# Hybrid sparse-attention and HGRN2 block: sums of x squares as 32-token products of one column, and ScalarE's order at three places

## What is computed

```python
def rms_norm(x, g):
    xf = x.astype(jnp.float32)
    y = xf * lax.rsqrt(jnp.mean(xf * xf, axis=-1, keepdims=True) + EPS)
    return (y * g.astype(jnp.float32)).astype(x.dtype)

mod = c_act @ w_ada[l] + b_ada[l]
shift1, scale1, gate1, shift2, scale2, gate2 = jnp.split(mod, 6, axis=-1)
h = rms_norm(x, norm1_g[l]) * (1.0 + scale1[:, None]) + shift1[:, None]
proj = h @ w_in[l]
(q_lat, a_k, a_v, k_idx, w_idx, b_q, b_f, b_i, b_g, gate_a, gate_b) = split_cols(proj, COL_SIZES)
q_lat = rms_norm(q_lat, q_lat_norm_g[l])
...
k_idx = rms_norm(k_idx, k_idx_norm_g[l])
...
h2 = rms_norm(x, norm2_g[l]) * (1.0 + scale2[:, None]) + shift2[:, None]
y = jnp.square(jax.nn.relu(h2 @ w_mlp1[l] + b_mlp1[l])) @ w_mlp2[l] + b_mlp2[l]
x = x + gate2[:, None] * y
```

## Time and profile before

| | before |
|---|---|
| median of 3 runs (lowest to highest), us | 771.15 (770.37 to 771.26) |
| the profiled execution's own time, us | 771.27 |
| its span, first to last instruction, us | 769.4 |
| TensorE busy | 761.0 us (99%) |
| VectorE busy | 630.9 us (82%) |
| ScalarE busy | 364.7 us (47%) |
| GpSimd busy | 62.7 us (8%) |
| moved by DMA | 95.50 MB, 124 GB/s on average |

### The profile page before, as it was taken

One profiled execution on the slowest core, in us unless ns is written; L12 is line 12 of the kernel. 1 busy time (PEld: TensorE's weight loads), 2 busy tenths in 40 slices (PEclk: granted clock), 3 DMA queues, 4 the chain that ended last, 5 costly groups with the idle time before them and its releaser, 6 DMA issues.

```text
span 769.4 us, 13224 instructions
## 1 busy us (share of the span) xinstructions
PE 761.0 (99%) x5208; PEld 645.8 (84%) x5208; DVE 630.9 (82%) x1129; ACT 364.7 (47%) x577; POOL 62.7 (8%) x64
## 2 busy tenths in 40 slices
PE   7999999999999999999999999999999999999998
PEld 6876878777878777778889988889999888889998
DVE  6975999778998677769966999879998766779996
ACT  5466524455344376654332555654333354454341
POOL 5015344200000000000012000000000000000000
PEclk9999999999999999999999999999999999999999
DMA  9943223221221233345556255312333433213331
GB/s 349 403 140 110 83 83 107 75 67 56 80 86 58 85 107 126 145 142 184 200 180 203 83 165 191 109 55 86 108 110 109 138 110 102 89 55 111 110 110 56
DMA packets 27643, 95.50 MB, mean 124 GB/s; under 512 B 3009, under 2 KB 3393, under 8 KB 27586
## 3 DMA queue, kind: packets, MB, share of 16 engines
q1 hardware_dynamic: 27296, 94.51, 36.8%
q10 hardware_dynamic: 290, 0.20, 0.1%
HBM read 92.61 MB, written 2.10 MB: 123 GB/s over the span
## 4 chain that ended last, share of the span: by engine, by line
PE 94%; DVE 3%; ACT 2%; issue 1%; DMA 1%; DVEq 0%; ACTq 0%
PE bank L1612 10%; PE bank L1614 10%; PE bank L1613 10%; PE bank L2187 7%; PE bank L2189 7%; PE bank L2188 7%; PE bank L1662 5%; PE bank L1841 2%; PE bank L1798 2%; PE bank L1842 2%; PE bank L1843 2%; PE bank L2015 2%; PE bank L1800 2%; PE bank L1799 2%; PE bank L2017 2%; PE bank L2016 2%
## 5 line engine op out<-in xcount | busy, mean ns | idle before, releaser
L1612 PE MATMUL bank<-h_hi,w_hi 128*128 128x512 f32 x328 | 128.2, 391 | 0.6 <-ACT relu_u L886 0.6
L1613 PE MATMUL bank<-h_lo,w_hi 128*128 128x512 f32 x328 | 127.7, 389 | 0.0
L1614 PE MATMUL bank<-h_hi,w_lo 128*128 128x512 f32 x328 | 127.6, 389 | 0.0
L526 ACT ACTIVATE w_hi<-w_raw 128x1024 fp32r<-128x1024 f32 (+2 forms) x94 | 97.4, 1039 | 30.7 <-PE bank L1819 9.4
L1087 DVE TENSOR_TENSOR w_lo<-w_raw,w_hi 128x1024 fp32r<-128x1024 f32 x68 | 83.5, 1236 | 11.7 <-ACT w_hi L526 11.7
L1612 PEld LDWEIGHTS bank<-h_hi,w_hi 128*128 128x128 f32 x328 | 61.6, 188 | 13.4 <-ACT relu_u L886 0.8
L2187 PE MATMUL bank<-u_hi,wf_hi 128*128 128x256 f32 x256 | 72.6, 284 | 0.1
L2189 PE MATMUL bank<-u_hi,wf_lo 128*128 128x256 f32 x256 | 72.4, 283 | 0.0
L2188 PE MATMUL bank<-u_lo,wf_hi 128*128 128x256 f32 x256 | 72.4, 283 | 0.0
L1614 PEld LDWEIGHTS bank<-h_hi,w_lo 128*128 128x128 f32 x328 | 61.6, 188 | 12.9
L1613 PEld LDWEIGHTS bank<-h_lo,w_hi 128*128 128x128 f32 x328 | 61.6, 188 | 12.6
(11 more groups left out here) (319 smaller groups left out, 1890.4 us busy)
## 6 DMA issues: line engine op xcount, KB each, us to landing
w_raw<-in_units SPq DMA_DIRECT2D x117, 512.0 KB, 3.3
ada_raw<-in_ada SPq DMA_DIRECT2D x16, 512.0 KB, 10.3
ada_even<-in_ada SPq DMA_DIRECT2D x16, 512.0 KB, 4.5
ada_odd<-in_ada SPq DMA_DIRECT2D x16, 512.0 KB, 4.4
w_raw<-in_units SPq DMA_DIRECT2D x8, 448.0 KB, 10.6
xT<-in_xt SPq DMA_DIRECT2D x4, 512.0 KB, 5.3
out<-xT SPq DMA_DIRECT2D x7, 256.0 KB, 2.5
w_raw<-in_units SPq DMA_DIRECT2D x1, 256.0 KB, 5.1
```

Source lines behind the costliest of these rows:

```text
L526: nc.scalar.activation(w_hi[:, s, 0:width], w_raw[:, s, 0:width], ACT.Copy).then_inc(hi_ready, 1)
L1612: mm(bank[b][:], w_hi[:, slot, j], rhs_hi(i), start=f, stop=False)
L1613: mm(bank[b][:], w_hi[:, slot, j], rhs_lo(i), start=False, stop=False)
L1614: end = mm(bank[b][:], w_lo[:, slot, j], rhs_hi(i), start=False, stop=l)
```

## The change

Four edits, in one.

1. The pair sums on VectorE go. Each slice's squares are summed by TensorE on their own, in 16 products of 32 tokens by one column of ones (row_sums), into four columns of bank 7; the root reads these four columns. Behind the first five slices stand two idle products each, behind the sixth one; the idle products behind the spread become seven.
2. VectorE squares slices 5 and 7, ScalarE the other six, and the table load for the root moves ahead of ScalarE's last square.
3. At the latents ScalarE makes both lat_hi, kw and kw_sq first and the latents' squares after these. VectorE's lat_lo now waits for lat_hi alone and its sum for both squares; TensorE waits for a square before it overwrites bank 0.
4. In the first half of the MLP the rounding of the first token-block sums moves from behind unit 1 to behind the relu of unit 2.

```diff
@@ -212,11 +212,12 @@
         ones_ready, consts_ready, consts_step = sem("ones_ready"), sem("consts_ready"), sem("consts_step")
         dve_own, act_own = sem("dve_own"), sem("act_own")
         lb_ready, gqk_ready = sem("lb_ready"), sem("gqk_ready")
-        xsq_ready, xsq_added, xsq_summed, xroot_ready, xspread = (
-            sem("xsq_ready"), sem("xsq_added"), sem("xsq_summed"), sem("xroot_ready"), sem("xspread"))
+        xsq_ready, xsq_made, xsq_summed, xroot_ready, xspread = (
+            sem("xsq_ready"), sem("xsq_made"), sem("xsq_summed"), sem("xroot_ready"), sem("xspread"))
         a1_ready, xn_ready, hfull_ready = sem("a1_ready"), sem("xn_ready"), sem("hfull_ready")
         slice_done, a_done = sem("slice_done"), sem("a_done")
         lat_ready, latsq_ready, latsq_added = sem("lat_ready"), sem("latsq_ready"), sem("latsq_added")
+        lathi_ready = sem("lathi_ready")
         kw_ready, kwsq_ready, k_taken = sem("kw_ready"), sem("kwsq_ready"), sem("k_taken")
         ki_summed, ki_root, ki_spread, ki_ready = (sem("ki_summed"), sem("ki_root"), sem("ki_spread"),
                                                    sem("ki_ready"))
@@ -297,6 +298,7 @@
 
             return (ada_odd if i % 2 else ada_even), i % 2, i // 2
 
+        X_ACT, X_DVE = (0, 1, 2, 3, 4, 6), (5, 7)
         LOGIT_BANK = [[6, 4, 2, 3], [6, 7, 4, 5]]
 
 
@@ -544,11 +546,10 @@
             x_square(3)
             c_sigmoid(1)
             x_square(4)
+            nc.scalar.activation(warm[:, 2:4], ident[:, 2:4], ACT.Sqrt)
             x_square(6)
-            x_square(7)
-            nc.scalar.activation(warm[:, 2:4], ident[:, 2:4], ACT.Sqrt)
-            act.wait_ge(xsq_summed, KC // 2)
-            nc.scalar.activation(XRS, bank[7][:, 0:T:P], ACT.Sqrt, scale=1.0 / D, bias=EPSC
+            act.wait_ge(xsq_summed, 1)
+            nc.scalar.activation(XRS, bank[7][:, 0:TB], ACT.Sqrt, scale=1.0 / D, bias=EPSC
                                  ).then_inc(xroot_ready, 1)
             split_hi(0, width=NA)
 
@@ -573,12 +574,14 @@
             for k in range(RC):
                 act.wait_ge(a_done, k + 1)
                 nc.scalar.activation(lat_hi[:, k], bank[k][:], ACT.Identity,
-                                     scale=col[:, V_QG + k:V_QG + k + 1])
-                nc.scalar.activation(sq[:, k], bank[k][:], ACT.Square).then_inc(latsq_ready, 1)
+                                     scale=col[:, V_QG + k:V_QG + k + 1]).then_inc(lathi_ready, 1)
             act.wait_ge(a_done, 3)
             nc.scalar.activation(kw[0:HD + IH, :], bank[2][0:HD + IH, :], ACT.Copy).then_inc(kw_ready, 1)
             act.wait_ge(t_lo, KC)
             nc.scalar.activation(kw_sq[0:HD, :], bank[2][0:HD, :], ACT.Square).then_inc(kwsq_ready, 1)
+            for k in range(RC):
+                act.wait_ge(lat_ready, k + 1)
+                nc.scalar.activation(sq[:, k], bank[k][:], ACT.Square).then_inc(latsq_ready, 1)
             act.wait_ge(slice_done, 7)
             split_hi(U_V + 1)
             for j in range(AC):
@@ -939,12 +942,14 @@
                     split_hi(U_1[1] + 3)
                 for j in range(MH - 2):
                     up_relu(h, j)
+                    if h == 0 and j == 2:
+                        tforms_hi(0, 0)
                     up_square(h, j)
                     if j < MH - WS:
                         split_hi(U_1[h] + WS + j)
                     if h == 0 and j >= KC:
                         out_bias(j - KC)
-                    if j % 2 and j < MH - 3:
+                    if j % 2 and j < MH - 3 and (h or j > 1):
                         tforms_hi(h, j // 2)
                 blocks_hi(h, 0)
                 tforms_hi(h, KC - 2)
@@ -997,10 +1002,10 @@
             v.tensor_tensor(LBC, col[:, V_LB:V_LB + BH], LBD, ALU.subtract)
             v.tensor_tensor(OML, col[:, V_LB + BH:V_LB + 2 * BH], LBD, ALU.subtract).then_inc(lb_ready, 1)
             v.tensor_tensor(GQK, col[:, V_HQ:V_HQ + 1], col[:, V_HK:V_HK + 1], ALU.mult).then_inc(gqk_ready, 1)
-            def x_add(p):
-
-                dve.wait_ge(xsq_ready, [2, 4, 5, 7][p])
-                v.tensor_tensor(x_sq[:, 2 * p], x_sq[:, 2 * p], x_sq[:, 2 * p + 1], ALU.add).then_inc(xsq_added, 1)
+            def x_square(k):
+
+                dve.wait_ge(x_loaded[k // 2], 16)
+                v.tensor_tensor(x_sq[:, k], xT[:, k], xT[:, k], ALU.mult).then_inc(xsq_made, 1)
 
             def c_product(j):
 
@@ -1008,14 +1013,10 @@
                 v.tensor_tensor(c_act[:, j * T:(j + 1) * T], c_sig[:, j * T:(j + 1) * T], bank[j][:],
                                 ALU.mult).then_inc(cact_ready, 1)
 
-            x_add(0)
             c_product(0)
-            x_add(1)
             c_product(1)
-            dve.wait_ge(x_loaded[2], 16)
-            step(v.tensor_tensor(x_sq[:, 5], xT[:, 5], xT[:, 5], ALU.mult))
-            x_add(2)
-            x_add(3)
+            for k in X_DVE:
+                x_square(k)
             dve.wait_ge(cact_ready, 2)
 
             def ada_dot1(i):
@@ -1061,11 +1062,12 @@
                     split_part(U_UQI, 4)
 
             for k in range(RC):
-                dve.wait_ge(latsq_ready, k + 1)
+                dve.wait_ge(lathi_ready, k + 1)
                 v.scalar_tensor_tensor(out=lat_lo[:, k], in0=bank[k][:], scalar=col[:, V_QG + k:V_QG + k + 1],
                                        in1=lat_hi[:, k].bitcast(F32), op0=ALU.mult, op1=ALU.subtract
                                        ).then_inc(lat_ready, 1)
             dve.wait_ge(t_lo, KC)
+            dve.wait_ge(latsq_ready, RC)
             v.tensor_tensor(lat_sq[:], sq[:, 0], sq[:, 1], ALU.add).then_inc(latsq_added, 1)
             dve.wait_ge(ki_root, 1)
             v.reciprocal(KRS, KRS).then_inc(ki_root, 1)
@@ -1643,17 +1645,21 @@
             for j in range(2):
                 mm(bank[j][:], ones[0:1, :], c_row[0:1, j * T:(j + 1) * T], start=True, stop=True
                    ).then_inc(c_spread, 1)
-            for p in range(KC // 2):
-                pe.wait_ge(xsq_added, p + 1)
-                for b in range(TB):
-                    t = slice(b * P, (b + 1) * P)
-                    end = mm(bank[7][:, t], x_sq[:, 2 * p, t], ones[:], start=p == 0 and b == 0,
-                             stop=p == KC // 2 - 1 and b == TB - 1)
-                end.then_inc(xsq_summed, 1)
+            for s, k in enumerate(X_ACT[:5]):
+                pe.wait_ge(xsq_ready, s + 1)
+                row_sums(7, 0, x_sq[:, k], P, s == 0, False)
+                idle_products(2)
+            pe.wait_ge(xsq_made, 1)
+            row_sums(7, 0, x_sq[:, X_DVE[0]], P, False, False)
+            idle_products(1)
+            pe.wait_ge(xsq_made, 2)
+            row_sums(7, 0, x_sq[:, X_DVE[1]], P, False, False)
+            pe.wait_ge(xsq_ready, len(X_ACT))
+            row_sums(7, 0, x_sq[:, X_ACT[5]], P, False, True).then_inc(xsq_summed, 1)
             idle_products(3)
             pe.wait_ge(xroot_ready, 2)
             row_spread(7, XRS).then_inc(xspread, 1)
-            idle_products(5)
+            idle_products(7)
 
 
             def a_pass(w, k, h, units, first=False, last=False):
@@ -1689,6 +1695,8 @@
             pe.wait_ge(lat_ready, RC)
             for m in range(2):
                 b = SCORE_BANK[m]
+                if b < RC:
+                    pe.wait_ge(latsq_ready, b + 1)
                 for i, j in enumerate((m, 2 + m)):
                     mm(bank[b][:], w_hi[:, U_UQI % WS, j], lat_hi[:, i], start=i == 0, stop=False)
                     mm(bank[b][:], w_hi[:, U_UQI % WS, j], lat_lo[:, i], start=False, stop=False)
```

## The result

The changed kernel took 775.87 us (median; 775.66 to 776.77) against 770.87 us for the kernel before on the same chip: a ratio of 1.0067, 95% interval 1.0052 to 1.0082. It is slower, by 5.0 us. The forecast was 771.0 us with a range of 768.8 to 773.4: the measured time lies above the range, and the forecast saw next to no change. The profiled execution took 776.77 us, 5.50 above the profiled execution of before; the spans (774.9 and 769.4) differ by the same 5.5.

A forecast was written before the change was run, and what follows sets the result against it. TensorE, busy 761.0 of the span's 769.4 us, was taken as the bound. Sums of squares +0.4, latents 0 and MLP -0.7 made -0.3 us on the profiled 771.27: 771.0 us, range 768.8 to 773.4.

The forecast's parts named there:

- a rise at about 9: Sums of squares: TensorE's clock goes from 1.2 to 2.4 GHz at about 9 us, against the old 12.2.
- The group at the slow clock: Sums of squares: one slice's 16 one-column products between idle products cost 0.56 us at 1.2 GHz, bounds 0.56 to 1.12.
- Five steps: Sums of squares: five times a group and its idle pair, each 1.01 us fast or 1.41 to 1.97 slow.
- The tail: End of the sums: a group, one idle product, a group and another directly behind it, 1.6 us together.
- S: Start of ScalarE's root behind the sums of squares: forecast at 13.6 us against 13.17, 0.4 us later, bounds -0.3 and +2.6.
- the second rival: Front: the clock stays at 1.2 GHz until the input products, S 15.1 to 19, +4 us, 774.6 us; chance 0.17.
- end 1 us after it: Behind the root: slow spread and seven slow idle products end 1 us after S + 3.39, the first input product's expected start.
- the prediction's own sign of being wrong: Front, in the changed kernel's trace: the prediction is wrong if S is below 12 or above 15.
- The squares: Front: square 6 is ready at about 10.5 us, before TensorE reaches it after 11.2, so squares do not delay the sums.
- The latents: ScalarE's new order: the 0.55 us pause goes but TensorE waits at the later spread instead; 0, bounds -0.7 and +0.2.
- The MLP: First MLP units: TensorE no longer waits for the relu of unit 2; -0.7 us, or -0.4 if entering the loop costs.
- The first rival: Front gains in earnest: the last square decides, S at 11.0, 2.2 us earlier, 768.4 us; chance 0.20.

The follow-up runs named there:

- e10: The changed kernel with sums as products of 128 tokens, ten idle products ahead of the eight groups and none among them; 780.00 us, ratio 1.0112 to the kernel before.
- e11: The changed kernel, its idle products kept, with each slice's sum as 4 products of 128 tokens; 784.56 us, ratio 1.0173 to the kernel before (two runs).
- e4: The changed kernel with ten idle products ahead of all eight groups and none among them; 777.30 us, ratio 1.0075 to the kernel before.
- e7: The changed kernel with slices 0 to 5 added in pairs on VectorE (five groups), ten idle products ahead, none among; 769.67 us, ratio 0.9979.
- e5: The changed kernel with ten idle products ahead of the groups and its own idle products left in place; 779.82 us, ratio 1.0105 (two runs).
- e1: The kernel before with only the edits at the latents and in the MLP, sums of squares as before; 770.42 us, ratio 0.9989.
- e2: The kernel before with only the edit at the latents; 770.86 us, ratio 0.9997.
- e9: The five groups of e7 with eight idle products ahead instead of ten; 770.26 us, ratio 0.9987 to the kernel before.
- e3: The changed kernel without the 11 idle products among the sums; 773.43 us, ratio 1.0027 to the kernel before.

## Why the prediction was wrong

**The step that failed is the clock.** The prediction took "a rise at about 9" for the sums, because TensorE no longer pauses at 6.2. It rose at 21.98, so all the sums ran at 1.2 GHz. What the reasoning leaned on, that TensorE is never idle, was not enough: in e10 and e11 it was never idle either. Every first rise on record in these runs came behind 128-column products without groups in between (from 6.03 in e4, from 6.37 in e7, from 17.89 in the change, from 24.39 in e11) or, in e5, with one group in them. In the kernel before, and in e1 and e2, the sums themselves were 128 columns wide, and the clock rose within them (12.19, 10.33 and 10.49); the change took those columns away, and the prediction did not ask what they had done for the clock besides their sums.

**The group at the slow clock** was put at 0.56 us, the low end of its bounds of 0.56 and 1.12. In the mixture it is 1.69 - 0.85 = 0.84, the middle. Back to back it is 0.43, so 0.4 of it goes with the changes of shape on both sides.

With the clock and the group as measured, and the start as it was, the sum of the prediction gives the profiled execution. Start 7.24 instead of 6.2: +1.04, the late row. Five steps of 1.69, 8.43, instead of two of 1.41 and three of 1.01, 5.85: +2.58. The tail from 15.67 to S, 2.36, instead of 1.6: +0.76. Together 4.4 later than its S of 13.6: 18.0. Then the spread and the idle products behind it, slow, put the first product 4.49 behind the root instead of 3.39: +1.1, the second rival's "end 1 us after it". In all 5.96 at the input products. The 1.04 is from one execution and not from the change; the median lies 0.9 under the profiled run.

**The second rival was the truth**, "the clock stays at 1.2 GHz", with S between 15.1 and 19 (18.03) and a price of +4 for 774.6 us (775.87). Its chance was 0.17. Both of its arguments came from rows, the one-row products that had not raised the clock and the lack of any row with a rise among one-column groups; the argument against it was the failed assumption. S above 15 was also the prediction's own sign of being wrong. The range took in a third of this rival and ended at 773.4.

**The squares** are no cover that ran out: the last ends at 10.57 for a forecast of 10.5. **The latents** are 0, for the reason given: the pause at the index sums goes (0.62 by the shift) and comes back at the spread; e2 shows it alone. **The MLP** is -0.72 for -0.7 in the trace of the change, and e1's ratio agrees (0.9989, a gain of 0.2 to 1.6 us by its interval). **The first rival**, a gain in earnest at 768.4, needed the clock up and no stop. No kernel here with eight groups of 32 tokens had both; with five groups e7 had S at 12.30 and the profiled run of e9 at 11.43, for the rival's 11.0.

The rule of the Trainium skill that the prediction gave no chance ("TensorE: Matmul & The Clock Gate", Part 1, a floor of about 25 ns from start to start) was not borne out here: e4's 199 records took 1.83 us, 9 ns each.

## What to carry to other kernels

When a change replaces wide products by narrow ones on TensorE, ask what the wide ones did for the clock: the prices of the rows at the fast clock hold only where something still raises it, and the one-column products here did not. Count instructions as well as time in the first microseconds: many short ones ran ahead of their own fetch here. And when an old cost falls by a factor, look at the next thing in line before spending the gain: here, with eight groups, the stop took it even at the fast clock (e4, e5).

## What the hardware showed that I had not expected

- One-column products of 128 tokens neither raised the clock nor held it, although TensorE was busy without a break: alternating with pairs of idle products they ran from 6.0 to 24.4 us at 1.2 GHz (e11), and alone they let it fall from 2.4 to 1.2 GHz at 15.39 (e10). The change's mixture of 32-token products and idle pairs, which did not raise it, did hold it, from 12.17 to past 16.6 us (e5).
- TensorE stopped behind 219 product records in e3, e4 and e5, for 1.86, 3.63 and 4.74 us, with "issue" as the only name for it, and went on about 2.4 us behind the start of an instruction packet.
- A one-column product of 128 tokens costs 213 ns a record at 1.2 GHz, as much as one of 128 columns; with 32 tokens it costs 13. With one column streamed in each case, its time went with the tokens of the loaded operand.
